# Routing arithmetic in bf16, expert biases inside the combine, V's remainders subtracted on VectorE, and two tiles of the tail's gating on GpSimd, in a one-core mixture-of-experts decoder step

## What is computed

```
h = layer_norm(ALPHA * x + gate1 * (merged @ w_o), ln1_g, ln1_b)
v = h * (1 + scale2) + shift2
logits = v @ w_router + b_router                # 32 experts
top_vals, top_idx = top_k(logits, 4)
gates = softmax(top_vals)
# for each token and each of its 4 experts e:
hid = v @ w_up[e] + b_up[e]                     # 2048 wide
act = min(glu, 7) * sigmoid(1.702 * glu) * (clip(lin, -7, 7) + 1)
f += gate * (act @ w_down[e] + b_down[e])
y = layer_norm(ALPHA * h + gate2 * f, ln2_g, ln2_b)
```

## Time and profile before

| | us |
|---|---|
| median of 3 runs | 1329.97 (1328.99 to 1330.07) |
| the profiled execution | 1328.42 |
| its span | 1326.6 |
| PE busy | 1218.2 (92%) |
| DVE busy | 564.0 (43%) |
| ACT busy | 230.1 (17%) |
| Pool busy | 149.4 (11%) |

### The profile page before, as it was taken

One profiled execution on the slowest core, in us unless ns is written; L12 is line 12 of the kernel. 1 busy time (PEld: TensorE's weight loads), 2 busy tenths in 40 slices (PEclk: granted clock), 3 DMA queues, 4 the chain that ended last, 5 costly groups with the idle time before them and its releaser, 6 DMA issues.

```text
span 1326.6 us, 17547 instructions
## 1 busy us (share of the span) xinstructions
PE 1218.2 (92%) x6199; PEld 523.0 (39%) x6200; DVE 564.0 (43%) x1062; ACT 230.1 (17%) x355; POOL 149.4 (11%) x90
## 2 busy tenths in 40 slices
PE   3899999867999999999989999999999999999980
PEld 0599964432333333333333333333333333333320
DVE  0617735865334343334334334343343433434346
ACT  0232200241111111111111111121111111111111
POOL 0367352074000000000000000000000000000003
PEclk8799999957999999999999999999999999999995
DMA  9744498645999999999996999998799999699941
GB/s 337 250 168 153 191 347 331 267 163 201 427 426 425 426 427 427 426 427 426 426 424 249 429 427 423 426 427 374 318 426 428 426 427 426 260 421 426 427 188 40
DMA packets 54708, 466.45 MB, mean 352 GB/s; under 512 B 5467, under 2 KB 5499, under 8 KB 18561
## 3 DMA queue, kind: packets, MB, share of 16 engines
q1 hardware_dynamic: 52817, 460.36, 84.2%
q0 software_dynamic: 1872, 5.84, 1.3%
HBM read 464.33 MB, written 1.85 MB: 351 GB/s over the span
## 4 chain that ended last, share of the span: by engine, by line
PE 66%; DMA 23%; DVE 7%; ACT 2%; issue 1%; SPq 1%; DVEq 0%; POOL 0%; ACTq 0%
PE bank L853 30%; DMA ring<-in_w_up 17%; PE bank L886 14%; PE bank L623 7%; PE bank L826 4%; PE bank L743 3%; DMA ring<-in_w_ada 3%; DMA hx<-in_x_sample 2%; PE bank L609 1%; PE bank L877 1%; ACT front L1016 1%; DMA mod_rows<-parts_home 1%; PE bank L845 1%; PE bank L782 1%; PE bank L811 1%
## 5 line engine op out<-in xcount | busy, mean ns | idle before, releaser
L853 PE MATMUL bank<-ring,front 128*64 128x512 f32 x2240 | 508.0, 599 | 14.9 <-DMA ring<-in_w_up 14.7
L853 PEld LDWEIGHTS bank<-ring,front 128*64 128x64 f32 x2240 | 151.2, 137 | 315.3 <-issue 285.1
L886 PE MATMUL bank<-ring,front 128*64 128x512 f32 x1120 | 248.0, 595 | 7.3 <-ACT front L1016 7.3
L1303 DVE TENSOR_TENSOR front<-front,bank 128x512 f32<-128x512 f32 (+1 forms) x210 | 143.6, 684 | 85.9 <-PE bank L826 73.2
L886 PEld LDWEIGHTS bank<-ring,front 128*64 128x64 f32 x1120 | 77.3, 137 | 153.8 <-issue 139.9
L1347 DVE TENSOR_TENSOR O_low<-bank,O_high 128x512 fp32r<-128x512 f32 x35 | 24.2, 691 | 244.3 <-ACT O_high L1019 244.3
L1013 ACT ACTIVATE front<-front 128x256 f32<-128x256 f32 x70 | 29.1, 416 | 546.4 <-DVE front L1321 546.4
L534 POOL TENSOR_TENSOR parts_home<-parts_home,front 128x1024 f32<-128x1024 f32 x2 | 4.7, 2373 | 992.1 <-ACT parts_home L948 992.1
L1321 DVE TENSOR_SCALAR front<-bank 128x256 f32<-128x256 f32 x70 | 29.7, 424 | 155.3 <-PE bank L853 154.1
L455 POOL TENSOR_TENSOR ring_parts<-ring,ring_parts 128x1024 fp32r<-128x1024 f32 x28 | 68.3, 2469 | 77.6 <-ACT ring_parts L919 77.6
L743 PE MATMUL bank<-parts_home,front 128*64 128x512 bf16 (+1 forms) x576 | 74.3, 389 | 0.0
(11 more groups left out here) (217 smaller groups left out, 961.7 us busy)
## 6 DMA issues: line engine op xcount, KB each, us to landing
ring<-in_w_up SPq DMA_DIRECT2D x128, 2048.0 KB, 17.4
ring<-in_w_down SPq DMA_DIRECT2D x128, 1024.0 KB, 16.8
ring<-in_w_ada SPq DMA_DIRECT2D x12, 2048.0 KB, 16.8
ring<-in_w_in SPq DMA_DIRECT2D x8, 2048.0 KB, 13.3
ring<-in_w_o SPq DMA_DIRECT2D x2, 2048.0 KB, 19.0
hx<-in_x_prompt SPq DMA_DIRECT2D x2, 1024.0 KB, 23.0
ring<-in_w_out_a SPq DMA_DIRECT2D x1, 2048.0 KB, 7.7
ring<-in_w_out_b SPq DMA_DIRECT2D x1, 2048.0 KB, 15.1
```

The costliest lines, as they stand in the source:

```text
L853: last = mm(bank[B_UP[j]][64 * h:64 * h + 64, :], x_T[:, (c % 2) * 2 + b, 64 * (c // 2):64 * (c // 2) + 64], w[:, :, at:at + 256], start=F ...
L886: last = mm(bank[B_DOWN][64 * h:64 * h + 64, :], act_T[:, 2 * j + b, 64 * hh:64 * hh + 64], expert_chunk_at(UP_CHUNKS + m)[:, b * 1024 + h ...
L1303: signal(TT(Y[0:r, 2 * t + h, :], Y[0:r, 2 * t + h, :], bank[b][0:r, :], ALU.add), bank_free[b], value)
```

## The change

- Constants: triangles and ones become bf16; the rank counts run in bf16 with a bf16 `mask`. Tile 2's rows stand twice, so that `rank` is one DVE instruction on 128 partitions, and the memsets and the subtraction of 1 go away (the slot numbers start at 1 instead).
- `mask` comes from one comparison with all four choices (`chosen`) and one reduction; the cast of the indices is done once.
- Normalisation: `v_rows` makes (hx - mean) * vec while ACT takes the root, and then times rstd plus offset. ACT's row pass (`norm_row`) is only for `hx` now.
- ACT's order: the v_T copies first, then `norm_row(2)`, the exponential, the first parts of V; the other six parts behind `xT_copy(0)`.
- Round 0's gather reads V itself in f32 with a one-hot `S_first` of its own, and waits for no part.
- The subtractions of V move from Pool to DVE, six in a row, behind `route_ready` and the two of `O_low` and ahead of DVE's loop.
- The six bias matmuls go away. b_down stands in the rows of `O_high`/`O_low` and the gates in `onehot_T` ahead of round 0, in high and low parts, so that round 0's `combine` gives their product; Pool clears `Y` instead of `O_high`, after the rank rows are written.
- `token_rows` moves behind `combine(g, 0)`, `add_up(g, 0)` ahead of the gate of the slots. `select_bias(0, 0)` and the wait for `route_ready` move.
- Tail: Pool gates tiles 1 and 2 as soon as the last round has written its one-hots, DVE tile 0; tile 2's last normalisation is done by DVE alone, like that of V.
- The banks of `B_X` and `B_T` change places.

```diff
-            def rest_of_v(t, q):
...
-            pool.memset(O_high[:, :].bitcast(F32), 0.0).then_inc(O_high_ready, 1)
+            pool.memset(onehot_T[:, :].bitcast(F32), 0.0).then_inc(cleared, 1)
+            pool.memset(O_low[:, :].bitcast(F32), 0.0).then_inc(cleared, 1)
+            pool.wait_ge(rank_rows_ready, 1)
+            pool.memset(Y, 0.0).then_inc(cleared, 1)
...
+            pool.wait_ge(onehot_ready, G + 1)
+            pool.wait_ge(bank_full[B_X], G + front_uses(B_X) + 1)
+            for i, t in enumerate((1, 2)):
+                pool.tensor_tensor(out_rows[0:r, t, :], Y[...], gate2, ALU.mult).then_inc(gated_ready, 1)
+                pool.tensor_tensor(out_rows[0:r, t, :], out_rows[0:r, t, :], hx[0:r, t, :], ALU.add).then_inc(sum_ready, 1)
...
-            gather(0)
+            pe.wait_ge(S_first_ready, 1)
+            for t in range(3):
+                for h in range(2):
+                    last = mm(bank[B_X][64 * h:64 * h + 64, :], S_first[0:ROWS[t], t, :], V[0:ROWS[t], t, h * 512:(h + 1) * 512],
+                              start=t == 0, stop=t == 2)
...
-                token_rows(g)
                 for c in range(UP_CHUNKS - 1):
...
                     if c < 2:
                         combine(g, c)
+                    if c == 0:
+                        token_rows(g)
...
+                row = V[0:r, t, :]
+                normalise(r, meanwhile=lambda: step(STT(row, hx[0:r, t, :], aggr[0:r, 0:1], vec[:, 2, :], ALU.subtract, ALU.mult)))
+                signal(STT(row, row, rstd[0:r, :], vec[:, 1, :], ALU.mult, ALU.add), v_ready, i + 1)
...
+            dve.wait_ge(cleared, 3)
+            dve.wait_ge(O_high_ready, 1)
+            for at in (0, 64):
+                low, raw, high = O_low[at:at + E, :], b_down_raw[at:at + E, :], O_high[at:at + E, :].bitcast(F32)
+                step(TT(low, raw, high, ALU.subtract)) if at == 0 else signal(TT(low, raw, high, ALU.subtract), O_low_ready, 1)
+
+            dve.wait_ge(bank_full[B_X], front_uses(B_X) + 1)
+            for i, (t, q) in enumerate(RESTS):
+                r = ROWS[t]
+                dve.wait_ge(v_part_ready, PARTS.index((t, q)) + 1)
+                signal(TT(V[0:r, t, :], V[0:r, t, :], v_parts[0:r, PART_AT[t][q], :], ALU.subtract), v_rest_ready, i + 1)
...
-                add_up(g, 0)
+                add_up(g, 0)
```

More of the change, by code:

```diff
@@ L174, in program @@
         hot = region(front, 6144, NT)
+        S_first = region(front, 7952, 3, SLOTS)
         S = region(front, 6472, 3 * SLOTS // 2).bitcast(BF16).rearrange("p (t s) -> p t s", t=3)
@@ L210, in program @@
         top_f = region(front, 17392, 3, 8)
[L211 removed]
+        mask = region(front, 17416, 3 * E // 2).bitcast(BF16).rearrange("p (t e) -> p t e", t=3)
         eq = region(front, 17512, 3, E)
@@ L216, in program @@
         count = region(front, 17803, 1)
-        rounds = region(front, 17804, 1)
+        rounds = region(front, 17804, 1).bitcast(BF16)[:, 0:1]
         bound = region(front, 17805, 1)
-        passed = region(front, 17806, NROUND)
+        passed = region(front, 17806, NROUND // 2).bitcast(BF16)
         base_f = region(front, 17870, NROUND)
@@ L939, in _, with root @@
                 free(name, AF(state_rows[0:r, i, :], ps[0:r, :], ACT.Copy))
-            def root(n, row):
-                r = row.shape[0]
+            def root(n, r):
                 if n:
@@ L997, in route_copy @@
                 ps = wait_full(act, name)
-                free(name, AF(route_T[0:3 * E, i, :], ps[0:3 * E, 0:NT], ACT.Copy))
+                free(name, AF(route_T[:, i, :], ps[:, 0:NT], ACT.Copy))
+            act.wait_ge(b_down_landed, 64)
+            AF(O_high[:, :], b_down_raw[:, :], ACT.Copy).then_inc(O_high_ready, 1)
+            ps = wait_full(act, "gate_T")
+            act.wait_ge(cleared, 1)
+            AF(onehot_T[:, 0:NT], ps[:, 0:NT], ACT.Copy).then_inc(gate_high_ready, 1)
             route_copy("gate_T", 1)
-            for i in range(6):
-                ps = wait_full(act, f"bias{i}")
-                r = ROWS[i // 2]
-                free(f"bias{i}", AF(Y[0:r, i, :], ps[0:r, :], ACT.Copy))
             route_copy("rank_T", 0)
@@ L1261, in _ @@
             ps = wait_full(dve, "rank")
-            step(v.memset(rank, -1.0))
-            for t in range(3):
-                r = ROWS[t]
-                ins = STT(rank[0:r, t, :], ps[0:r, t * E:(t + 1) * E], 1.0, mask[0:r, t, :], ALU.add, ALU.mult)
-                step(ins) if t < 2 else free("rank", ins)
-            for t in range(3):
-                step(TS(rank[0:ROWS[t], t, :], rank[0:ROWS[t], t, :], -1.0, None, ALU.add))
-            step(v.tensor_copy(rank[NS_TOK:P, 2, :], rank[0:NS_TOK, 2, :]))
-            step(v.tensor_copy(copies(0), each_copy(rank)))
+            free("rank", STT(rank, ps[:, 0:3 * E].rearrange("p (t e) -> p t e", t=3), 1.0, mask, ALU.add, ALU.mult))
+            first_slots = rank_of_slot[:, 0:SLOTS].unsqueeze(1).to_broadcast([P, 3, SLOTS])
+            signal(TT(S_first, first_slots, by_slot(rank[:, :, 0:1]), ALU.is_equal), S_first_ready, 1)
             ps = wait_full(dve, "bounds")
@@ L1273, in _ @@
             signal(TS(passed[0:E, :], iota[0:E, 0:NROUND], bound[0:E, :], None, ALU.is_ge), passed_ready, 1)
-            one_hots(0, 0, 0)
+            signal(v.tensor_copy(copies(0), each_copy(rank)), rank_rows_ready, 1)
             ps = wait_full(dve, "table")
```

216 lines of the change are left out of this document (111 added, 105 removed).

## The result

Over the four runs of each kernel that were timed beside each other, the changed kernel took 1315.11 us (1313.43 to 1317.70) and the kernel before 1329.48 (1328.73 to 1330.07): a ratio of 0.9894, 95% interval 0.9874 to 0.9914. The profiled execution took 1313.43 us, its span is 1311.6; that of before was 1328.42 and 1326.6. So the two profiles to be compared lie 15.0 us apart.

A forecast was written before the change was run, and what follows sets the result against it. The DMA weight stream was taken to set the first long stretch. Front 9.6, rounds 0 and tail 4.6 sum to 14.2 us off the profiled 1328.42: 1314.2, plus 1.55 for the median, 1315.8; range 1300 to 1324.

The forecast's parts named there:

- DVE's time up to add_up(0, 0): Rank rows to the end of add_up(0,0) in round 0: 34.8 us, ending at 311.0; bounds 21.8 and 38.2.
- v_ready, mask, rank rows: Normalisation and routing ahead of round 0: last v_ready at 264.3 us, mask at 272.2, rank rows at 276.2.
- Chunk 0: First chunk of round 0 starts at about 285.5 us, 26.5 earlier, after an f32 gather of 4.4 us.
- The turns: DVE's splitting, O_low and V subtractions: nearly each instruction waits for one of Pool's nine on hx, 16.5 us for nine.
- Strictly in turn: Order of DVE and Pool instructions running side by side ahead of round 0: one of DVE's, one of Pool's.
- The front by the stream: Front measured by when the weight stream runs without a hole: load after chunk 2 at 318.5 us, not 328.1; gain 9.6.
- In the rounds: token_rows behind the first combine, add_up ahead of the gate instructions: same instructions, 0 us.
- Rival (3): Slower: bf16 token_rows between f32 groups costs each PE-bound round; at 2 us a round +6, 1336 us; chance 0.05.
- Tail: Behind the last down-projection: gating on Pool and DVE 3.7 us earlier, last normalisation 0.9; 4.6 us taken.
- Rival (1): No collision on DVE ahead of round 0: add_up(0,0) at 298.0, gain 29.7, kernel at 1300.3 us; chance 0.12.
- Rival (2): Gain eaten: all nine Pool instructions in front, half clock through chunk 3, tail at lower bound; gain 7.7, 1322.3; chance 0.10.
- (4): Rounds start no earlier as add_up(0,0) ends as late as now; little of the tail remains: 1328 to 1332; chance 0.03.

The follow-up runs named there:

- before_tail: The kernel before with the new tail alone (Pool gates tiles 1 and 2, DVE tile 0, one pass less at the end): 1323.69 us, 0.9968.
- h_in_downs: The changed kernel with Pool's hx work done one token tile under each of the down-projections of rounds 0 to 2: 1308.18 us, 0.9843.
- subs_late_h_downs: The changed kernel with V subtractions on Pool behind O_low, hx work in the down-projections of rounds 0 to 2, Y cleared before the rank rows: 1302.56 us, 0.9796.
- after: The changed kernel itself, in its first runs and profile: 1315.11 us, 0.9894 to the kernel before.
- pool_subs: The changed kernel with the V subtractions given back to Pool, after round 0's gather and ahead of its hx work: 1317.40 us, 0.9934.
- all_parked: subs_late_h_downs with Pool's loads for the tail made to wait for round 13's one-hots: 1295.51 us, 0.9752.
- before_tokens: The kernel before with only the order inside rounds changed: token_rows behind combine(g,0), add_up(g,0) ahead of the gate: 1326.01 us, 0.9975.

## Why the prediction was right, and what in it was not

The forecast of 1315.8 was 0.7 us above the first median, and the later two of the same code (1317.87 unaltered, 1317.82 with its tail loads parked) lie in the range. The gain was 14.4, 10.1 and 11.1 us in the three sessions, so that the 14.2 forecast lies at the upper end.

That it met the first session is in part luck. Counted from the landing of `mod_rows` that DVE waits for, the three profiles of this code gain 12.5, 11.2 and 11.2 us on that of before, where the forecast had 9.6 for the front, 0 for the rounds and 4.6 for the tail. The front gives 6.1, 6.3 and 6.5, the rounds 1.65, 0.1 and -0.1, the tail 4.8 in each. The mechanism was right. The term that was mis-sized is DVE's time up to add_up(0, 0), 3.4 us short, and it is what the front lacks; in the first profile 2.5 us of an early landing and 1.65 us in the rounds made up for it. The kernel before is less steady in that stretch than the new one: from the landing to the rank rows it takes 53.65 us in its own profile and up to 55.32 with the same front (before_tail), so these gains could be up to 1.7 us larger. By its steps:

- **v_ready, mask, rank rows.** Forecast 264.3, 272.2, 276.2; measured 262.06, 270.38, 274.40, in an execution whose landing was 2.46 us early. With that added: 264.5, 272.8, 276.9. Right, each to 0.7 us.
- **Chunk 0** at 284.24 (286.7 with the 2.46), forecast 285.5. The f32 gather took 5.15 us, not 4.4.
- **The turns.** The mechanism and its place were right: Pool started on hx 8.2 us behind the rank rows (forecast 8.0), and the subtractions start 3.27 us apart where tiles of 128 rows meet. The size was short: add_up(0, 0) ended 38.2 us behind the rank rows, not 34.8, the bound given for all nine Pool instructions in front, and all nine were. Without any of them it is 24.0 (h_in_downs) where the undisturbed sum had 21.8. 2.06 of those 2.2 us are the table's tensor_scalar, which sat out the clearing of Y: 2.24 for 0.18. That is the case weighed from the Trainium skill ("SBUF — State Buffer", Who interferes with whom: a DVE instruction in a 2-port mode against any GpSimd instruction, whoever came first); the trace agrees, 2.24 us beside the memset and 0.18 without, and the hint taken against it, two-input instructions beside memsets, did not bear on it. The turns themselves were put at 13.0 (34.8 - 21.8) and took 14.2, 1.2 more. 2.2 and 1.2 are the 3.4 us of the step that failed. That the bound and the measured time are the same 38.2 us is chance: the bound had 21.8 and 16.4 for the nine, the runs have 24.0 and 14.2. The terms listed for the splitting, 1.9, 0.35, 0.9 and 4.8, add up to 7.95 and not to the 7.5 used; the 7.5 was right (7.47 from the rank rows to the end of the splitting in subs_late_h_downs, where nothing stands beside it). The rank rows ended 1.8 us earlier than forecast in the first profile and hid half of the 3.4; in the two others of this code they ended at 277.20 and 275.81 instead of 274.40, with the same 38.3 and 38.2 us behind them. "Strictly in turn" held for the instructions with two inputs here, and not for every cast (2.52 us in after, 6.46 in pool_subs).
- **The front by the stream**, not by round 0. The successor of chunk 2 was issued at 319.52, forecast 318.5; the front gained 8.55, forecast 9.6, and 6.1 of the 8.55 without the early landing. The measure held to 0.7 us (382.2 to 383.4) in every kernel whose tail loads lay outside the stream. The prediction said that of a moved step every DMA counts; here it didn't ask where Pool's loads for the tail would land, and they happened to fall in the hole.
- **In the rounds**: forecast 0, measured 1.65 us in the first profile, 0.1 and -0.1 in the two others. The new order takes 0.15 us from each PE-bound round, and the rounds that wait for weights can take all of it back. Rival (3), a price there, has the sign wrong.
- **Tail**: forecast 4.6, measured 4.8 in all three profiles and 4.25 alone. DVE's first product waited for Pool's last (2.94 for two of 0.71 each), 1.5 us of the 1.7 forecast; the pass at 1301.07 stood against L552 of Pool, as the earlier trace rows had it.
- **Rival (1)** was refuted for this kernel, but its time was right as the price of the collision: 1300.3 for a kernel without it; 1302.05 was measured with hx moved away and the loads parked. **Rival (2)** was half true: all nine Pool instructions lay in front, but the clock was back at 1.00 from 318 us on, so that chunk 2 alone was slow. **(4)** fell.

The version without turns in the front and with the loads parked, all_parked, is 1295.51 us, 33.5 below before and 19.6 below the changed kernel's first median. Its stream runs unbroken from 290 us.

What stays open: why the landing of `mod_rows` varies by 2.8 us (231.50 to 234.26) from execution to execution; the start of the second output projection varies by 4 us, but the rank rows follow the landing and not that. How much Pool's subtractions would gain with the tail's loads parked and the queues still side by side was not run. And no run tells how far the loads of the tail cost more than their bytes because of their size or because of the queue that they come from.

## What to carry to other kernels

When an instruction with two SBUF inputs moves to DVE, look at what Pool has queued in that stretch, since each of Pool's costs DVE a wait (1.6 us on the mean here) that goes by the length of Pool's instruction; that of DVE's hardly matters. Moving the work back to Pool brought add_up(0, 0) forward by only 4.3 us as long as the two queues overlapped; putting them one behind the other took the waits away. Measure a front by when the saturated DMA stream runs without a hole, and then ask of every side load where it falls: 1.8 MB were free in a hole and 6 to 7 us inside the stream. A gain that equals the forecast in one session may hold an execution's luck of 2.5 us, which shows when the two traces are compared from the last wait ahead of the change; repeat it before each term of the sum is called confirmed.

## What the runs showed of the hardware that was not expected

- 1.8 MB in eleven loads of Pool's queue, 4.2 us at 427 GB/s, cost the weight stream 6 to 7 us; while they ran the DMA share stayed at 1.02 and the rate fell from 424 to 389 GB/s over 30 us, to 291 in the worst eight (378 to 386 us in subs_late_h_downs).
- A tensor_scalar on one partition of 64 elements took 2.24 us beside Pool's memset of 128x3072, a cast of 32x640 took 6.46 us beside Pool's V subtractions of 2.33 us each, and the six subtractions of 7.50 us took 17.09 beside six of Pool's.
- A reordering of the same instructions inside a round, 0.45 us of bf16 matmuls from ahead of chunk 0 to behind the combine, shortened the round by 0.17 us (before_tokens, which also moves add_up).
